# A two-layer mixture-of-experts trunk: expert weights in 2 MB pieces through a ring of eight places

## What is computed

```
for i in range(2):
    h = h + (attention if i == 0 else gated_short_conv)(rms_norm(h))
    xt = rms_norm(h)                         # 512 x 1024
    ...                                      # router: 2 of 32 experts for each token, with gates
    for e in range(32):                      # tokens of expert e: xb
        g, u = split(xb @ w_gate_up[i, e], 2)        # 1024 x 1024, 4 MB
        y    = (silu(g) * u) @ w_down[i, e]          # 512 x 1024, 2 MB
    h = h + sum over a token's two experts of gate * y
return rms_norm(h)
```

## Time and profile before

| | |
|---|---|
| three runs | 1452.12, 1453.46, 1456.77 us; median 1453.46 |
| the profiled execution | 1453.89 us, of which the span from first to last instruction is 1452.2 us |
| TensorE matmul busy | 1280.6 us, 88% of the span |
| VectorE, ScalarE, GpSimd busy | 405.7, 336.3, 133.2 us |
| weights of the experts | 134 DMAs: 62 of 4 MB, 8 of 1 MB, 64 of 2 MB |
| DMA in all | 456.01 MB, 314 GB/s over the span |
| experts of layer 0, TensorE | 240.4 to 704.8 us |
| experts of layer 1, TensorE | 957.6 to 1423.7 us |

### The profile page before, as it was taken

One profiled execution on the slowest core, in us unless ns is written; L12 is line 12 of the kernel. 1 busy time (PEld: TensorE's weight loads), 2 busy tenths in 40 slices (PEclk: granted clock), 3 DMA queues, 4 the chain that ended last, 5 costly groups with the idle time before them and its releaser, 6 DMA issues.

```text
span 1452.2 us, 15480 instructions
## 1 busy us (share of the span) xinstructions
PE 1280.6 (88%) x6014; PEld 688.8 (47%) x6014; DVE 405.7 (28%) x867; ACT 336.3 (23%) x632; POOL 133.2 (9%) x109
## 2 busy tenths in 40 slices
PE   5968897998999989999489998799999989999991
PEld 4844675443344333433168877654343433443330
DVE  5376232111111111111455454321111211111114
ACT  3249321221112111221231121212111211121112
POOL 5070020010000000000000000201000100000000
PEclk9978997999999999999779999889999999999996
DMA  9200227999999999999722232479999999999974
GB/s 353 72 1 1 116 115 291 436 429 427 432 432 430 428 429 435 429 429 402 270 60 88 87 118 114 200 318 425 428 434 429 431 428 431 433 429 430 427 298 196
DMA packets 55497, 456.01 MB, mean 314 GB/s; under 512 B 13924, under 2 KB 29310, under 8 KB 38308
## 3 DMA queue, kind: packets, MB, share of 16 engines
q1 hardware_dynamic: 44084, 444.29, 73.0%
q0 software_dynamic: 5120, 8.41, 1.5%
q10 hardware_dynamic: 6256, 2.80, 0.8%
HBM read 444.96 MB, written 18.90 MB: 319 GB/s over the span
## 4 chain that ended last, share of the span: by engine, by line
PE 54%; DMA 35%; DVE 6%; ACT 4%; issue 1%; SPq 0%; POOLq 0%; DVEq 0%; ACTq 0%
DMA big<-in_moe_w_gate_up_dram 33%; PE ps L1015 22%; PE ps L834 19%; PE ps L1033 5%; PE ps L993 3%; DVE xr L1154 1%; PE ps L938 1%; ACT arena L659 1%; ACT arena L675 1%; PE ps L820 1%; PE ps L1005 1%; DVE arena L1249 1%; PE ps L914 1%; DVE h L1293 1%; DVE h L1291 1%
## 5 line engine op out<-in xcount | busy, mean ns | idle before, releaser
L1015 PE MATMUL ps<-big,arena 128*64 128x512 f32 x2048 | 470.5, 615 | 49.8 <-DMA big<-in_moe_w_gate_up_dram 47.3
L1015 PEld LDWEIGHTS ps<-big,arena 128*64 128x64 f32 x2048 | 151.3, 142 | 362.7 <-issue 293.6
L1375 DVE TENSOR_TENSOR gain<-arena,ps 64x512 f32<-64x512 f32 x64 | 68.5, 1070 | 458.8 <-ACT arena L721 458.8
L721 ACT ACTIVATE arena<-ps 64x512 f32<-64x512 f32 x64 | 37.7, 589 | 530.5 <-PE ps L1015 530.5
L540 POOL DMA_INDIRECT rows<-arena x64 | 62.4, 975 | 912.5 <-DVE arena L1401 912.5
L1033 PE MATMUL ps<-small,arena 128*64 128x512 f32 x512 | 116.9, 598 | 0.0
L834 PE MATMUL ps<-xt_parts,small_parts 128*128 128x512 f32 x288 | 112.2, 399 | 1.5 <-DVE xr_parts L1163 1.5
L834 PE MATMUL ps<-xr_parts,small_parts 128*128 128x512 f32 x272 | 107.3, 394 | 0.0
L834 PE MATMUL ps<-xt_parts,big_parts 128*128 128x512 f32 x256 | 100.1, 391 | 0.0
L993 PE MATMUL ps<-arena_parts 128*128 128x512 f32 x256 | 85.5, 416 | 0.0
L993 PE MATMUL ps<-xr_parts,arena_parts 128*128 128x512 f32 x256 | 81.4, 400 | 0.0
(11 more groups left out here) (156 smaller groups left out, 1271.0 us busy)
## 6 DMA issues: line engine op xcount, KB each, us to landing
big<-in_moe_w_gate_up_dram SPq DMA_DIRECT2D x62, 4096.0 KB
small<-in_moe_w_down_dram SPq DMA_DIRECT2D x32, 2048.0 KB, 19.3
arena<-in_moe_w_down_dram SPq DMA_DIRECT2D x16, 2048.0 KB, 18.4
xt<-in_moe_w_down_dram SPq DMA_DIRECT2D x16, 2048.0 KB, 17.8
big<-in_conv_w_in_dram SPq DMA_DIRECT2D x12, 1024.0 KB, 9.2
big<-in_moe_w_gate_up_dram SPq DMA_DIRECT2D x8, 1024.0 KB, 17.6
big<-in_attn_w_qkv_dram SPq DMA_DIRECT2D x1, 4096.0 KB
big<-in_attn_w_o_dram SPq DMA_DIRECT2D x1, 4096.0 KB
```

The source lines that it names most:

```text
L721: nc.scalar.activation(silu[BLOCK:P, j, :], ps[2 + j][0:BLOCK, :], ACT.Silu).then_inc(S.silu_ready, 1)
L1015: mm = nc.tensor.matmul(ps[2 + j][half * BLOCK:(half + 1) * BLOCK, :], xg[:, k, j * BLOCK:(j + 1) * BLOCK], w[:, k, half * FF:(half + 1) * ...
L1375: V.tensor_tensor(hid[BLOCK:P, j, :].rearrange("q (k p) -> q p k", p=P), silu[BLOCK:P, j, :].rearrange("q (p k) -> q p k", p=P), ps[2 + j] ...
```

## The change

The gate-up and down places of a layer become one ring of eight places of 2 MB (`ring[l]`): the four halves of `big`, the two of `small`, `late` and `xt`. A gate-up matrix is two pieces (steps 0 to 3 and 4 to 7 of the contraction), a down matrix is one, so that a pair has six pieces, a layer 96. SP loads them in the order of use: gate-up 0 first and second half, gate-up 1 first and second half, down 0, down 1, then the next pair. Piece n waits until piece n-8 is used. `gate_up` now does one half, waits for that half alone, and counts up `gu_done` by one (so twice an expert; `swish` waits for 2n+2). SP's loop is written out: 96 DMAs and waits a layer. TensorE's loop has four pairs per turn, three turns, and the last four pairs are written out. In layer 0 the first three pieces, with `late` among them, wait for `pT_ps`. The convolution's first quarter, which goes into `big[0]`, waits for `down_done` 30 (the last use of `big[0]` in layer 0 is by pair 14's down matrices) and not for the 31st gate-up.

```
-        def load_experts(l, big_free, small_free):
...
+        halves = [[big[:, s, 0:FT], big[:, s, FT:DT]] for s in range(BIG_SLOTS)]
+        ring = [[*halves[0], late_slot, *halves[1], small[:, 0], small[:, 1], xt_slot],
+                [*halves[1], *halves[0], small[:, 0], small[:, 1], late_slot, xt_slot]]
+        def ring_loaded(eng, l, m, q, c):
+            at = q * PIECES + c
+            eng.wait_ge(ring_in[at % RING], m * (GROUP * PIECES // RING * 16)
+                        + (at // RING + 1 + l * PAIRS * PIECES // RING) * 16)
...
+            def load_experts(l):
+                early_free = [(pT_ps, 4 * TT * KV)] * 3 + [(mix_ps, 2 * TT)] * 4 + [(logits_ps, TT)] if l == 0 else \
+                    [(gates_ps, DT)] * 2 + [(mix_ps, 4 * TT)] * 5 + [(logits_ps, 2 * TT)]
+                for i in range(PAIRS):
+                    for c in range(PIECES):
+                        n = i * PIECES + c
+                        if n < RING:
+                            sp.wait_ge(*early_free[n])
+                        else:
+                            before, used = divmod(n - RING, PIECES)
+                            if used < 4:
+                                sp.wait_ge(main[l].gu_done, 4 * before + used + 1)
+                            else:
+                                sp.wait_ge(main[l].down_done, 2 * before + used - 4 + 1)
+                        if c < 4:
+                            w = w_gate_up[l, 2 * i + c // 2].rearrange("(p k) n -> p k n", p=P)[:, c % 2 * FT:(c % 2 + 1) * FT]
+                        else:
+                            w = w_down[l, 2 * i + c - 4].rearrange("(p k) n -> p k n", p=P)
+                        sp.dma_start(ring[l][n % RING], w).then_inc(ring_in[n % RING], 16)
...
-                    sp.wait_ge(main[0].gu_done, E - BIG_SLOTS + q + 1)
+                    sp.wait_ge(*[(main[0].down_done, E - 2), (main[0].gu_done, 2 * E - 1)][q])
...
-                act.wait_ge(S.gu_done, n + 1)
+                act.wait_ge(S.gu_done, 2 * n + 2)
...
+            def gate_up(S, j, part, w):
+                for a in range(FT):
+                    k = part * FT + a
...
+                def up(m, q, j):
+                    for part in range(2):
+                        ring_loaded(pe, l, m, q, 2 * j + part)
+                        gate_up(S, j, part, slot(q, 2 * j + part))
...
+                with pe.Fori(0, PAIRS // GROUP - 1) as m:
+                    for q in range(GROUP):
+                        pair(m, q)
+                for q in range(GROUP):
+                    pair(PAIRS // GROUP - 1, q, last=(q == GROUP - 1))
```

More of the change, by code:

```diff
@@ L203, in build_trunk @@
         w_out_in = sem("w_out_in")
-        last_in = [[sem(f"last_in{l}{q}") for q in range(LAST_CUTS)] for l in range(L)]
-        big_in = [sem(f"big_in{s}") for s in range(BIG_SLOTS)]
+        ring_in = [sem(f"ring_in{s}") for s in range(RING)]
+        query_in = sem("query_in")
+        w_o_in = sem("w_o_in")
         kv_in = sem("kv_in")
@@ L286, in build_trunk @@
         QC = D // QUARTERS
[L287 to L306, removed]
+        halves = [[big[:, s, 0:FT], big[:, s, FT:DT]] for s in range(BIG_SLOTS)]
+        late_slot = late.rearrange("p a b c -> p (a b) c")
+        xt_slot = xt[:].rearrange("p (a b) c -> p a (b c)", a=FT)
+        ring = [[*halves[0], late_slot, *halves[1], small[:, 0], small[:, 1], xt_slot],
[4 more added lines that the diff above has]
+                        + (at // RING + 1 + l * PAIRS * PIECES // RING) * 16)
         CONV_SPLIT = DT
@@ L388, in load_experts_over @@
                 sp.nop()
[L390 to L402, removed]
@@ L1007, in turn_picked @@
                 mm.then_inc(S.gathered, 1)
[L1009 to L1013, removed]
+            def gate_up(S, j, part, w):
+                for a in range(FT):
+                    k = part * FT + a
                     for half in range(2):
                         mm = nc.tensor.matmul(ps[2 + j][half * BLOCK:(half + 1) * BLOCK, :],
-                                              xg[:, k, j * BLOCK:(j + 1) * BLOCK], w[:, k, half * FF:(half + 1) * FF],
+                                              xg[:, k, j * BLOCK:(j + 1) * BLOCK], w[:, a, half * FF:(half + 1) * FF],
                                               start=(k == 0), stop=(k == DT - 1))
@@ L1043, in experts @@
                 turn_picked(S, 0)
[L1045 to L1054, removed]
-                    down_loaded(pe, l, m, odd, j)
-                    down(S, (m * 2 + odd) * 2 + j, j, down_slot(odd, j))
@@ L1075, in experts, with slot @@
-                up(PAIRS - 1, 0)
-                gate_up(S, 1, big[:, big_slot(b0 + 1)], last_in[l])
-                pe.wait_ge(S.where_ready, PAIRS)
-                for j in range(2):
-                    turn(PAIRS // 2 - 1, 1, j)
-                    finish(PAIRS // 2 - 1, 1, j)
+                def slot(q, c):
+                    return ring[l][(q * PIECES + c) % RING]
+                def up(m, q, j):
+                    for part in range(2):
+                        ring_loaded(pe, l, m, q, 2 * j + part)
+                        gate_up(S, j, part, slot(q, 2 * j + part))
@@ new lines, in finish, with pair @@
+                def finish(m, q, j):
+                    ring_loaded(pe, l, m, q, 4 + j)
+                    down(S, (m * GROUP + q) * 2 + j, j, slot(q, 4 + j))
+                def pair(m, q, last=False):
+                    i = m * GROUP + q
+                    pe.wait_ge(S.rows_taken, i * 2 + 2)
+                    up(m, q, 0)
+                    up(m, q, 1)
+                    pe.wait_ge(S.where_ready, i + 1)
+                    turn_hidden(S, i * 2, 0)
+                    if not last:
+                        pick(S, i + 1)
+                    finish(m, q, 0)
+                    turn_hidden(S, i * 2 + 1, 1)
+                    if not last:
+                        turn_picked(S, i + 1)
+                    finish(m, q, 1)
@@ L1093, in experts @@
                                 for j in range(2):
-                                    gate_up(over[l], j, big[:, j])
+                                    for part in range(2):
+                                        gate_up(over[l], j, part, halves[j][part])
                                 for j in range(2):
```

45 lines of the change are left out of this document (13 added, 32 removed).

## The result

| | median | range of runs |
|---|---|---|
| before | 1455.12 us | 1452.12 to 1457.76 (4 runs) |
| changed | 1431.96 us | 1431.32 to 1433.70 (4 runs) |

The ratio is 0.9847, 95% interval 0.9825 to 0.987: 23.2 us faster. Forecast were 26.4 us and 1427, with a range of 1418 to 1437.

What follows compares the result with a forecast made beforehand. The prediction took a full DMA stream to bound the expert stages, leaving only its ends to win: 28.4 - 1.5 - 0.5 = 26.4 us off the profiled 1453.9 gave 1427.5, median forecast 1427, range 1418 to 1437.

Steps and rivals of the forecast that it cites:

- rival of the quarter: End of layer 0: convolution's quarter delays the last piece up to 7.5 us or scatters pay 5.7; 1431 to 1435, chance 0.09.
- What bounds: Expert stages: a full DMA stream at 29.97 us a pair, TensorE with 2.9 us to spare; only the ends can gain.
- Start, 3.4 us a layer: Start of each expert stream: first place free after half a gate-up, so the stream starts and ends 3.4 us earlier.
- thin margins of 1.7 and 1.3 us: First pairs of a stream: releases come 1.7 and 1.3 us before they are needed, so the stream has no pause.
- End: End of each expert stage: only one down product of 3.67 us follows the last piece; 13.4 and 15.1 us earlier, start included.
- More DMAs, taken as 0: Expert streams: 96 DMAs a layer instead of 67, 58 more in both, their fixed cost hidden by queuing; 0 us.
- row for nothing: Loading ahead of small, late and xt, 2 MB at a time: share 1.03 at 439 GB/s, evidence that more DMAs cost nothing.
- a step above 30.1 us at a share below 1.0: Full expert stream: sign that the forecast is wrong and each DMA has a cost.
- Finer waits: TensorE in the expert stages: six waits a pair instead of four lie in slack; fewer clock dips, 0.5 us for both layers.
- The quarter and the scatters, 1.5 us: End of layer 0: the last two scatters meet the convolution's first quarter; 1.5 us lost, bounds 0 and 5.7.
- the 7 that the prediction had named as a sign of being wrong: TensorE's end in layer 0 to the first split of the convolution's weights: more than 7 us, 4.9 before.
- Loops written out: TensorE's doubled loop body and SP's written-out loop: waits for instructions are recovered in slack; 0 us.

Runs made afterwards that it cites:

- e3: Changed kernel, but a half of a gate-up place is given free only when the whole matrix has been used; 1439.05 us, ratio 0.9892.
- e9: Changed kernel with the first release after a quarter of the first matrix, with a 1 MB DMA for it; 1432.50 us, ratio 0.9855.
- e2: Kernel before, with only the last pair's down matrices loaded after the last gate-up matrices; 1454.14 us, ratio 0.9994.
- e1: Changed kernel with each 2 MB piece of layer 1 brought by two DMAs of 1 MB; 1439.52 us, ratio 0.9888.
- e8: Changed kernel's halves in before's places and order, the convolution's first quarter waiting for a gate-up again; 1449.80 us, ratio 0.9970.
- e4: Changed kernel without the load of the convolution's first quarter, 3 MB left out, for its trace alone; 1430.38 us (one run).
- e5: Changed kernel with neighbouring pieces of layer 1 joined into 4 MB DMAs, first release after a whole matrix; 1439.68 us, ratio 0.9893.

## Why the prediction came out as it did

It was right, within its range and 3.2 us short of the forecast's gain. The median of 1432 also lies where the prediction put its rival of the quarter, 1431 to 1435, so the time alone doesn't tell the two apart; the traces do, and they find parts of the shortfall in two places. Its steps in turn.

**What bounds.** Right. The expert stages are a full stream at a fixed step, and only its ends moved.

**Start, 3.4 us a layer.** Right: 3.6 by the issue (7.27 - 3.69), 3.3 and 3.4 by e3. The thin margins of 1.7 and 1.3 us held; e9 met the first one.

**End.** The sizes were nearly right, TensorE's end 3.7 us behind the last landing as foretold, but the reason given for before's 13.6 us was only half of it. I read them as the rest of the last gate-up and both downs. Those make 11.1 us; what set the end was TensorE's work of 43.6 us from pair 14's landing. e2, which this reading promised 19 us, measured none. The forecast didn't suffer, because the change lifts both limits. That was luck: the prediction asked only whether the last pair would be ready in time, and never what held TensorE before it.

**More DMAs, taken as 0.** This is the term that was mis-sized. The streams, from first issue to last landing, took 687.68 - 241.79 = 445.9 us and 1398.14 - 952.61 = 445.5, against 691.2 - 247.7 = 443.5 and 443.4: 2.4 and 2.1 us more for 29 more DMAs a layer, 0.07 to 0.08 each, and e1 gives 0.06. Together 4.5 us. e8 has it with before's order too (445.7 us in layer 0), so it isn't the order. My row for nothing, 439 GB/s over 5 us, was too short for a difference of half a per cent. Of the sign that I had named for it, a step above 30.1 us at a share below 1.0, the step came (30.12 to 30.18) and the share didn't (1.01). The Trainium skill's fixed cost ("DMA: Bandwidth & Descriptors", on the anatomy of one DMA, about 2.0 us, fitted there to DMAs that GpSimd issues) is not what an additional DMA of SP costs in a full queue: by these runs a thirtieth of it.

**Finer waits.** Right, better than expected. Two waits of 1.3 us a pair in place of one that was often 2.8 to 3.2: the granted clock over 1000 to 1380 us is 1.00, every half gate-up behind a wait took 3.65 to 3.68 us at the higher level, and the 0.5 us I had set aside weren't needed.

**The quarter and the scatters, 1.5 us.** Measured 5.59 - 3.17 = 2.4, and e4 shows the cause. From TensorE's end to the first split it was 7.3 us, just over the 7 that the prediction had named as a sign of being wrong: this half of the rival came true, at less than half of its 5.7. The other half, that the quarter holds up the last pieces, is out. Between this and layer 1's first gate-up the changed kernel took another 2.3 us more than before (250.2 against 248.0). That stretch lay between 247.8 and 250.2 us in all profiles, of kernels that don't touch it too, so I don't count it to the change; a cause for it I can't name.

**Loops written out.** Right, nothing: no wait for instructions above 1.5 us in `gate_up`. (The 100 us of the earlier trace rows are 1.7 turns of the loop of two pairs, 60 us each, and not three.)

With the measured sizes the sum is 7.2 (start) + 21.5 (end: TensorE's end 13.6 and 15.3 us behind the last landing before, 3.7 in both layers now) - 4.5 (DMAs) - 2.4 (scatter) = 21.8 us. The spans fell by 21.6; the 2.3 us gained ahead of the first gate-up and the 2.3 lost in the convolution cancel. The medians fell by 23.2.

## What to carry to other kernels

Where a stage is a full stream, price its ends. It ends at the later of two limits: the last transfer plus what is done with it, and the last transfer that the engine really waits for plus all its work from there. Loading in the order of use, through the whole stage and not only at its end, lifts both, and lifting one alone can measure as nothing. Make pieces fine where they shorten the first release or the last use, and coarse in between, as long as the coarse ones don't delay a release or a last use (e5 lost more that way than it gained): each additional DMA in a full queue costs something, here 0.06 to 0.08 us, that no share of busy time shows.

## What the runs showed of the hardware

A DMA share of 1.01 stands for 430, 428 or 421 GB/s, with 4, 6 or 12 DMAs for the same bytes; the share can't tell them apart. SP's three issues of the convolution's quarter took 22.7 us with a full queue ahead of them, against 3.1 at the stream's end in before: the sequencer stands in the issue itself, as no wait lies between the three. Here nothing was behind it. And with the same order and places, e8's two waits a pair, most of 1.2 to 1.6 us, kept the granted clock over 1000 to 1380 us at 1.00, where before, with one wait of 0.8 to 3.2 us a pair, had 0.97: 11 of its 22 waits were followed by a gate-up of 8.4 to 10.1 us in place of 7.09. Not every long wait did it; behind one of the longest, at 1168.95 us, the gate-up took 7.11.

The scatters move less than the kernel's description and the prediction say: 8.41 MB went through their queue in 64 scatters, 0.13 MB each on the mean and not 0.26.
